# Routing seven of eight token tiles while the last tile is still in the mixers

## The chip, the core and the metric

The kernel runs on one core of a Trainium2 chip. The metric is the device time of one execution in microseconds. The engines are named as in the profile: PE (matmul), PEld (its weight loads), DVE (vector), ACT (scalar), POOL (GpSimd), SP (the engine that issues most DMAs); "q" behind a name is its sequencer.

## What is computed

One layer over 1024 prompt tokens and 8 sample tokens, width 1024, float32. The trunk: norm, one input projection to 3740 columns, three groups of recurrent heads, output projection, residual. Then a mixture of experts: the reference's router takes the best of 4 groups and in it the best 2 of 8 experts, each a SwiGLU of width 256.

```python
h2 = _rms_norm(x, norm2_g[li]).reshape(b * l, D_MODEL)
pg = jax.nn.softmax((x @ rg_w + rg_b).astype(F32), axis=-1)   # x is h2 here
pg_top, g_idx = lax.top_k(pg, 1)
le = (x @ re_w + re_b).astype(F32).reshape(t, N_GROUPS, EXP_PER_GROUP)
...
v2, i2 = lax.top_k(pe, TOP_K)
```

The experts' outputs, weighted by the gates, are added to x, and a last norm follows.

## The kernel before

**Trunk.** The 1024 tokens go through in 8 tiles (0 to 7) of 128. The engines' programs are written by hand, with a semaphore for each step. `body(t)` of each engine does tile t's mixers and, woven into them, the input projection of tile t+1 (`unit`) and what is left of tile t-1: output projection (`project_out`), `residual`, `norm2`, the transposes of the normed rows (`turn_h2`, `put_h2T`), the router's matmul (`route`) and its bias (`logits`), which leaves 36 logits per token in `lg`. In tile 7 there is no next tile; its loop over levels (`order`, with steps P, lin and TU) passes between PE, DVE, ACT and POOL. The 8 sample tokens go along, in tile 7 under names in `_s`. Behind `body(7)` stand tile 7's own output projection, residual, norm, transposes, router and the store of its normed rows (`store_h2`) to `h2_d` in HBM. All engines then meet at a barrier.

**Routing.** In `experts`, a first block starts the weights of experts 0 to 3 on SP and routes all 9 tiles at once on DVE, with `then` after nearly each instruction (it waits for its own result): `first_max` finds a first maximum in five instructions; one-hot rows `oh`; counts and positions of each token within its expert by matmuls with triangular and all-one matrices (L2065 to L2071); experts ranked by their count; the rank's place looked up (L2177 to L2181); an address of each token-slot; one-hots of tile and row (L2205 to L2209), and 18 matmuls (L2094) that scatter the token numbers into a table, `tokens`.

**Experts.** 23 "quads" of 128 slots hold the ranked experts: the first 8 ranks have 128 slots each, the next 12 have 96, the last 12 have 64; what goes beyond is left to a loop of overflow tiles at the end, whose number DVE puts into a table in `overflow_table` during quad 1. For each quad POOL gathers rows from `h2_d` (L2249), PE transposes them (L2405), multiplies by w1 and w3 (`mm1`, L2416), DVE and ACT form the gated hidden rows, PE turns them (L2423) and multiplies by w2 (`mm2`, L2435), POOL scatters to `y2_d`. SP waits for the first two gathers, then loads the experts' weights of ranks 4 to 31 in order into 7 buffers, each as soon as the quads that used it are done. A last phase adds the two outputs per token, norms and stores.

## Time before and its profile

| | |
|---|---|
| runs | 1418.8, 1418.57, 1414.5 us; median 1418.57 us |
| profiled execution | 1419.8 us, of which the span shown is 1418.0 us |
| PE busy in the span | 1253.5 us (88%) |
| DVE busy | 636.3 us (45%) |
| ACT, POOL busy | 396.9 us (28%), 472.0 us (33%) |
| granted PE clock, mean | 0.932 of full |

Times in the rows are microseconds from the span's start. The trunk lasts to about 1035, routing to 1073, the quads to 1371, the last phase to 1418. A share near 1.00 in the column "DMA share" means that all 16 DMA engines are taken.

### The profile page before, as it was taken

The numbers are of one execution on the slowest core, as the hardware profiler recorded it, in microseconds if no ns is written. First come the engines' busy times: TensorE is split into PE (matmuls) and PEld (weight loads), VectorE is DVE, ScalarE is ACT, GpSimd is POOL, SyncE is SP. The second block draws the span as 40 slices with busy tenths as digits, with TensorE's granted clock in tenths as the row PEclk, the third lists the DMA queues.
The fourth block names the chain that finished last, engine by engine and source line by source line (L and its number), as shares of the span: only waits on it lengthen the run. The fifth ranks groups of instructions, "written<-read, shape, count | busy, mean of one in ns | idle before, by whom it ended". The sixth has DMA issues, their size and how long they took to land. (4 is left out here: it accounts for less than half of the span.)

```text
span 1418.0 us, 32185 instructions
## 1 busy us (share of the span) xinstructions
PE 1253.5 (88%) x13694; PEld 951.6 (67%) x13694; DVE 636.3 (45%) x1372; ACT 396.9 (28%) x832; POOL 472.0 (33%) x398
## 2 busy tenths in 40 slices
PE   7988899999999999999999999978645999998860
PEld 6778689879879978978987978756533333333320
DVE  2748763355256246246245444445353322222228
ACT  3233134234234224223423422322100222221113
POOL 1615582372264145336238238233001111111100
PEclk9999999999999999999999999967857999999985
DMA  9887637836935844853873662580076979999968
GB/s 270 266 222 213 194 98 242 253 106 197 282 122 166 274 128 151 264 186 106 250 230 106 201 197 85 180 90 19 13 312 262 359 304 413 416 417 416 395 228 318
DMA packets 217735, 317.28 MB, mean 224 GB/s; under 512 B 15332, under 2 KB 187952, under 8 KB 209000
## 3 DMA queue, kind: packets, MB, share of 16 engines
q1 hardware_dynamic: 205176, 277.51, 59.0%
q10 hardware_dynamic: 5792, 20.78, 4.3%
q0 software_dynamic: 6624, 16.92, 3.1%
q8 instruction: 110, 1.80, 0.6%
q14 instruction: 33, 0.27, 0.1%
HBM read 295.45 MB, written 27.01 MB: 227 GB/s over the span
## 5 line engine op out<-in xcount | busy, mean ns | idle before, releaser
L1566 PE MATMUL psum<-arena 128*128 128x256 f32 (+3 forms) x1536 | 309.7, 355 | 3.4 <-issue 3.4
L1566 PEld LDWEIGHTS psum<-arena 128*128 128x128 f32 x1536 | 253.9, 193 | 32.6 <-issue 4.1
L2416 PE MATMUL psum<-arena 128*64 128x512 f32 (+1 forms) x832 | 169.3, 619 | 8.1 <-DMA arena<-in_exp_w 8.1
L1562 PE MATMUL psum<-arena 128*128 128x128 f32 x1152 | 138.9, 281 | 3.6 <-DVE arena L1104 3.6
L1248 DVE COPY_PREDICATED arena<-arena,psum 128x128 f32<-128x128 int32 x280 | 85.7, 306 | 120.6 <-PE psum L1749 113.6
L1562 PEld LDWEIGHTS psum<-arena 128*128 128x128 f32 x1152 | 134.3, 196 | 6.3 <-issue 5.8
L674 POOL TENSOR_TENSOR arena<-arena 128x768 f32<-128x768 f32 (+1 forms) x32 | 59.2, 1850 | 197.9 <-ACT arena L902 197.9
L2416 PEld LDWEIGHTS psum<-arena 128*64 128x64 f32 (+1 forms) x832 | 51.9, 135 | 108.4 <-issue 106.1
L1836 PE MATMUL psum<-arena 128*128 128x256 f32 x512 | 117.5, 389 | 0.8 <-ACT arena L979 0.8
L1836 PEld LDWEIGHTS psum<-arena 128*128 128x128 f32 x512 | 98.8, 196 | 14.8 <-ACT arena L979 1.2
L2258 POOL DMA_INDIRECT y_d<-arena x23 | 23.0, 1002 | 221.8 <-DVE arena L2357 221.8
L2435 PE MATMUL psum<-arena 128*64 128x512 f32 (+1 forms) x416 | 83.2, 594 | 0.8 <-DVE arena L2374 0.8
L2363 DVE TENSOR_SCALAR arena<-psum 128x256 f32<-128x256 f32 x23 | 9.8, 425 | 154.3 <-PE psum L2416 154.3
L748 ACT ACTIVATE arena<-psum 128x256 f32<-128x256 f32 (+2 forms) x72 | 25.1, 348 | 179.3 <-PE psum L1566 179.3
L616 POOL TENSOR_TENSOR arena<-arena 128x1152 f32<-128x1152 f32 x24 | 67.0, 2792 | 1.9
L1749 PE MATMUL psum<-arena 32*64 32x64 f32 (+1 forms) x2400 | 60.9, 232 | 6.9 <-DVE arena L1248 6.2
L658 POOL TENSOR_TENSOR arena<-arena 128x768 f32<-128x768 f32 x8 | 16.5, 2068 | 139.5 <-DVE arena L1187 139.5
L1749 PEld LDWEIGHTS psum<-arena 32*64 32x64 f32 (+1 forms) x2400 | 49.6, 139 | 19.3 <-issue 8.8
L2435 PEld LDWEIGHTS psum<-arena 128*64 128x64 f32 (+1 forms) x416 | 25.6, 131 | 54.6 <-issue 53.6
L638 POOL TENSOR_TENSOR arena<-arena 128x384 f32<-128x384 f32 x16 | 18.0, 1142 | 129.6 <-DVE arena L1142 129.6
L2291 ACT ACTIVATE arena<-arena 128x256 f32<-128x256 f32 x23 | 9.6, 416 | 173.4 <-DVE arena L2363 173.4
L1506 PE MATMUL psum<-arena 64*64 64x64 f32 x1344 | 50.4, 229 | 6.1 <-DVE arena L1265 6.1
(402 smaller groups left out, 2025.1 us busy)
## 6 DMA issues: line engine op xcount, KB each, us to landing
arena<-in_w_in SPq DMA_DIRECT2D x96, 1024.0 KB, 6.5
arena<-in_exp_w SPq DMA_DIRECT2D x96, 1024.0 KB, 16.6
arena<-in_w_out SPq DMA_DIRECT2D x32, 1024.0 KB, 5.8
arena<-in_w_in SPq DMA_DIRECT2D x24, 512.0 KB, 5.0
arena<-y_d SPq DMA_DIRECT2D x16, 512.0 KB, 12.2
arena<-in_x_prompt ACTq DMA_DIRECT2D x15, 512.0 KB, 6.1
arena<-in_w_in SPq DMA_DIRECT2D x8, 576.0 KB, 4.7
arena<-in_w_in SPq DMA_DIRECT2D x8, 560.0 KB, 4.3
```

Source lines behind the costliest of these rows:

```text
L616: g.tensor_tensor(cv3, cv3, part, ALU.add).then_inc(step("tap" if i < 3 else "conv"), 1)
L674: g.tensor_tensor(near_z(zk[dt % 2][R, :]), near(e), near_qk(k), ALU.mult)
L748: ins = a(columns(w if w < QKV0 else w - CONV, n), src[:, 0:n], ACT.Copy)
L1248: ins = v.copy_predicated(h3(att_b)[:, h:h + 2, :], b3(q_mask[4 * half + j], 2, 64), new)
L1506: ins = mm(out[HALF[b ^ cross], 64 * h:64 * h + 64], lhs(h, b), rhs(h, b), start=True, stop=True)
L1562: ins = mm(b[:, j * P:(j + 1) * P], w[:, c, j * P:(j + 1) * P], hT[:, c, :], start=(c == 0), stop=(c == KC - 1))
L1566: ins = mm(b[:, 0:n], hT[:, c, :], w[:, c, 0:n], start=(c == 0), stop=(c == KC - 1))
L1749: ins = mm(bank[6 + i][HALF[b], 64 * j:64 * j + 64], left[R, at:at + 64], right[R, at:at + 64], start=True, stop=True)
L1836: ins = mm(bank[6 if b else 3][:, WIDE * (m % 2):WIDE * (m % 2) + WIDE], oT[:, c * P:c * P + P], w[:, c, :], start=(c == 0), stop=(c == KC ...
L2258: pool.indirect_dma_start(y2_d, bass.IndirectOffsetOnAxis(ap=idx[q % NX][1], axis=0), Y[q % NX], None, bounds_check=2 * (NT * P + NS) - 1, ...
L2416: ins = mm(bank[2 + q % 2][at:at + width, :].rearrange("p (m n) -> p m n", m=2), xT[q % 2][:, c, at:at + width], w13[n % NB][:, :, c, :], ...
L2435: ins = mm(bank[4 + 2 * (q % 2) + b][at:at + width, :], hT[q % 2][:, c * P + at:c * P + at + width], w2[n % NB][:, c, 512 * b:512 * b + 51 ...
```

## The change

- The router's matmul takes the rows before the norm: norm2_g is multiplied into the router's weights at the start (with its loads cut in halves, three more small DMAs), and `logits` multiplies by the row's reciprocal root. `turn_h2` transposes x2, not h2, so it no longer waits for the norm. At the end of the trunk `norm2(7)` comes behind the transposes on DVE and ACT.
- Tiles 0 to 6 and the sample tokens are routed during tile 7: first choices and second choices, total, keys, ranks, tables, positions, look-up, addresses, one-hots, in nine places of DVE's program, with their matmuls in four places of PE's. Experts are ranked by these tokens alone.
- Behind the barrier only tile 7's tokens are routed and placed, on top of what the psum banks hold. The table has 96 tiles, not 64, and a slot of tile 7 beyond its expert's room makes 32 more overflow tiles run. SP no longer waits for `by_rank`.

```diff
-OVER = 32
+SLOT_TILE = list(range(NT - 1)) + [NT, NT - 1]
+EARLY = NTT - 1
+OVER_EARLY = (2 * ((NT - 1) * P + NS)) // (2 * TS + 1)
+OVER = OVER_EARLY + N_EXP
 TILES = NQ + OVER
+TAB = 96
+assert TILES <= TAB
...
+PICK = (4, 8, 8, 8, 8, 1, 1)
+def first_max(v, then, iota, n, out, ap, k, top, cand, mi):
+    c = t3(cand[:, 0:n * k], k)
+    then(v.tensor_reduce(top, ap, AX, ALU.max))
+    then(v.tensor_tensor(c, ap, spread(top, k), ALU.is_ge))
+    then(v.scalar_tensor_tensor(c, c, -64.0, spread(iota[:, 0:k], n, 1), ALU.mult, ALU.add))
+    then(v.tensor_reduce(mi, c, AX, ALU.min))
+    then(v.tensor_tensor(t3(out, k), c, spread(mi, k), ALU.is_equal))
+def pick_first(v, then, lg, iota, n, best, scratch, tmp):
...
+    first_max(v, then, iota, n, ohk0, t3(sel, 8), 8, best, cand, mi)
+def pick_second(v, then, lg, iota, n, oh, second, scratch):
...
+    then(v.scalar_tensor_tensor(sel, ohk0, -1e30, sel, ALU.mult, ALU.add))
+    first_max(v, then, iota, n, ohk1, t3(sel, 8), 8, second, cand, mi)
+    oh4 = oh.rearrange("p (t k e) -> p t k e", k=2, e=32)
+    for k, ohk in enumerate((ohk0, ohk1)):
+        ins = tt(oh4[:, :, k, :].rearrange("p t (g e) -> p t g e", e=8), spread(t3(ohk, 8), 4, 2),
+                 spread(t3(ohg, 4), 8, 3), ALU.mult)
+    then(ins)
+    return lambda d4: tt(t3(d4, 4), lg[:, :, 0:4], spread(mx, 4), ALU.subtract)
+def look_up(v, then, n, words, oh, tabs, tmp, uw, uw_i, parts_i, parts):
+    w = n * words
+    for j in range(words):
+        ins = v.tensor_tensor(t3(tmp[:, 32 * n * j:32 * n * j + 32 * n], 32), t3(oh, 32), spread(tabs[:, 32 * j:32 * j + 32], n, 1), ALU.mult)
+    then(ins)
+    then(v.tensor_reduce(uw, t3(tmp[:, 0:32 * w], 32), AX, ALU.add))
+    then(v.tensor_copy(uw_i, uw))
+    v.tensor_scalar(parts_i[:, 0:w], uw_i, PACK - 1, None, ALU.bitwise_and)
+    then(v.tensor_scalar(parts_i[:, w:2 * w], uw_i, PACK.bit_length() - 1, None, ALU.logical_shift_right))
+    then(v.tensor_copy(parts, parts_i))
...
+def addresses(v, then, n, pos, parts, columns, addr_i, place_i, place, late=None):
+    tt, ts, stt = v.tensor_tensor, v.tensor_scalar, v.scalar_tensor_tensor
+    far, over, addr, step_up, past, idx, more, shift = pieces(columns, *[n] * COLUMNS)
+    if late is None:
+        first, second, cap32, ovb = pieces(parts, *[n] * 4)
+    else:
+        first, second, behind, cap32, ovb, n_early = pieces(parts, *[n] * 6)
+    ts(far, pos, float(2 * TS), None, ALU.is_gt)
...
+    if late is not None:
+        stt(more, n_early, float(P), idx, ALU.mult, ALU.is_lt)
+    stt(step_up, step_up, -float(2 * TS), far, ALU.add, ALU.mult)
+    then(stt(past, ovb, float(P), idx, ALU.mult, ALU.add))
+    if late is not None:
+        stt(shift, behind, -1.0, more, ALU.add, ALU.mult)
+    then(tt(addr, addr, step_up, ALU.add))
+    if late is not None:
+        v.tensor_reduce(late, more, AX, ALU.add)
+        then(stt(past, shift, float(P), past, ALU.mult, ALU.add))
+    then(stt(past, past, float(NQ * P), addr, ALU.add, ALU.subtract))
+    then(tt(past, past, over, ALU.mult))
...
+    then(v.tensor_copy(place, place_i))
...
-                     (rw_g, A["router_g_w"][0].rearrange("(p c) n -> p (c n)", c=KC)),
-                     (rw_e, A["router_e_w"][0].rearrange("(p c) n -> p (c n)", c=KC))]
+                     (g2c.rearrange("p (b c) -> p b c", b=2), A["norm2_g"][0].rearrange("(b p c) -> p b c", b=2, c=KC // 2))]
+            for b in range(2):
+                half = slice(D // 2 * b, D // 2 * b + D // 2)
+                loads += [(rw_g[:, 16 * b:16 * b + 16], A["router_g_w"][0, half].rearrange("(p c) n -> p (c n)", c=KC // 2)),
+                          (rw_e[:, P * b:P * b + P], A["router_e_w"][0, half].rearrange("(p c) n -> p (c n)", c=KC // 2))]
...
             def norm2(t):
                 done(act, "x2", t)
                 freed(act, "h2", t)
+                freed(act, "lg", t)
...
             put_oT(NT - 1)
+            put_h2T(NT - 1)
             norm2(NT - 1)
             store_x2(NT - 1)
-            put_h2T(NT - 1)
             store_h2(NT - 1)
             for name in ("x2_stored", "tail_stored"):
...
+                if last:
+                    early_first(0, EARLY - 2)
+                    early_second(0, EARLY - 2)
...
                     if what == "lin":
+                        if last and m == 0:
+                            early_first(EARLY - 2, EARLY)
+                        if last and m == 4:
+                            early_second(EARLY - 2, EARLY)
+                            early_total()
+                        if last and m == 6:
+                            early_keys()
+                        if last and m == 7:
+                            early_ranks()
+                        if last and m == 9:
+                            early_tables()
...
+                if last:
+                    early_positions()
...
+                if last:
+                    look_up(v, then, E2, 2, e_oh, tabs, e_pair, e_uw, e_uw_i, e_parts_i, e_parts)
...
-                tt(lg[:, 36 * t:36 * t + 36], bank[7][:, 0:36], rb, ALU.add).then_inc(step("lg"), 1)
+                v.scalar_tensor_tensor(lg[:, 36 * slot_of(t):36 * slot_of(t) + 36],bank[7][:, 0:36], st2[:, 2:3], rb, ALU.mult, ALU.add).then_inc(step("lg"), 1)
...
+            def early_first(a, b):
+                if b == EARLY:
+                    done(dve, "s_lg", 0)
+                pick_first(v, then, lg3[:, a:b, :], iota, b - a, best[:, a:b], e_scratch[:, 0:sum(PICK) * (b - a)], e_tmp)
+            def early_second(a, b):
+                scratch = e_scratch[:, 0:sum(PICK) * (b - a)]
+                oh = e_oh[:, 64 * a:64 * b]
+                gap = pick_second(v, then, lg3[:, a:b, :], iota, b - a, oh, second[:, a:b], scratch)
+                oh4 = oh.rearrange("p (t k e) -> p t k e", k=2, e=32)
+                if b == EARLY:
+                    then(ts(oh4[:, b - a - 1, :, :], oh4[:, b - a - 1, :, :], cum[:, NS - 1:NS], None, ALU.mult))
+                tt(t3(e_S[:, 32 * a:32 * b], 32), oh4[:, :, 0, :], oh4[:, :, 1, :], ALU.add)
+                then(gap(d4[:, 4 * a:4 * b]))
+            def early_total():
+                v.tensor_reduce(e_total, e_S.rearrange("p (t e) -> p e t", e=32), AX, ALU.add).then_inc(step("e_total"), 1)
+            F = slice(0, N_EXP)
+            key_col, rank, cap, n_ov, ex_col, n_ex = (e_cols[F, n:n + 1] for n in range(6))
+            def early_keys():
+                done(dve, "e_count_mm", 0)
+                v.scalar_tensor_tensor(key_row[F, :], bank[4][F, 32:64], 32.0, key_lead[F, :], ALU.mult, ALU.add)
+                then(cp(n_ex, bank[4][F, 0:1]))
+                then(v.scalar_tensor_tensor(key_col, n_ex, 32.0, lead_col[F, :], ALU.mult, ALU.add))
...
+                then(v.tensor_reduce(n_ov, ovm[F, :], AX, ALU.add))
+                ts(ovT[F, :], ones[F, :], n_ov, None, ALU.mult)
+                ts(ovT_b[F, :], ones[F, :], n_ov, -float(PACK), ALU.mult, ALU.mult)
+                then(ts(ovT_p[F, :], ones[F, :], n_ov, float(PACK), ALU.mult, ALU.mult))
...
+            def early_positions():
+                for b in range(2):
+                    T4 = slice(half * b, half * b + half)
+                    for k in range(2):
+                        ins = tt(tmp4[:, T4, k, :], oh4[:, T4, k, :], t3(bank[4 + b][:, 384:512], 32), ALU.mult)
+                then(ins)
+                then(v.tensor_reduce(e_pos, t3(e_tmp, 32), AX, ALU.add))
+                dve.sem_inc(step("e_pos"), 1)
+            def early_hot():
+                tile3, slot3 = t3(e_tile_hot, TAB), t3(e_slot_hot, P)
+                then(tt(tile3, spread(iota[:, 0:TAB], E2, 1), spread(e_place[:, 0:E2], TAB), ALU.is_equal))
+                tt(tile3, tile3, spread(dst_f[:, 0:E2], TAB), ALU.mult)
+                for half in range(2):
+                    N = slice(EARLY * half, EARLY * half + EARLY)
+                    tt(slot3[:, N, :], spread(iota, EARLY, 1), spread(e_place[:, E2 + N.start:E2 + N.stop], P), ALU.is_equal
+                       ).then_inc(step("e_hot"), 1)
...
             put_oT(NT - 1)
+            addresses(v, then, E2, e_pos, e_parts, e_columns, e_addr_i, e_place_i, e_place)
+            early_hot()
             residual(NT - 1, 0)
             residual(NT - 1, 1)
+            put_h2T(NT - 1)
             norm2(NT - 1)
-            put_h2T(NT - 1)
             logits(NT - 1)
             done(dve, "lg", NT - 1)
...
+                        if last and m == 3:
+                            early_counts()
+                        if last and m == 4:
+                            early_positions()
+                        if last and m == 5:
+                            early_tables()
...
+            def early_counts():
+                done(pe, "e_total", 0)
+                mm(bank[4][F, 0:1], e_total, ones[:, 0:1], start=True, stop=True)
+                mm(bank[4][:, 32:64], ones, e_total, start=True, stop=True).then_inc(step("e_count_mm"), 1)
+            def early_positions():
+                half = EARLY // 2
+                done(pe, "e_above", 0)
+                for b in range(2):
+                    o, at = bank[4 + b][:, 384:512], 32 * half * b
+                    mm(o, cum, e_S[:, at:at + 128], start=True, stop=False, skip_group_check=True)
+                    for i in range(half * (b + 1) - 1):
+                        n = max(i + 1 - half * b, 0)
+                        mm(o[:, 32 * n:128], ones, spread(e_S[:, 32 * i:32 * i + 32], half - n, 1), start=False,
+                           stop=(i == half * (b + 1) - 2), skip_group_check=True)
+                mm(bank[4][F, 64:96], ones[F, F], above[F, :], start=True, stop=True).then_inc(step("e_rank_mm"), 1)
+            def early_tables():
+                done(pe, "e_rank", 0)
+                mm(bank[5][:, 0:32], first_b[F, :], of_rank[F, :], start=True, stop=True)
...
+                mm(bank[5][0:1, P:P + 32], e_cols[F, 4:5], ident[F, F], start=True, stop=True).then_inc(step("e_tabs_mm"), 1)
+            def early_places():
+                done(pe, "e_pos", 0)
+                done(pe, "oc_dn", NT - 1)
+                mm(bank[5][:, 0:32], ones, e_total, start=True, stop=False, skip_group_check=True)
+                for n in range(E2):
+                    done(pe, "e_hot", 0, n // EARLY + 1)
+                    mm(bank[4][0:TAB, 0:P], e_tile_hot[:, TAB * n:TAB * n + TAB], e_slot_hot[:, P * n:P * n + P],
+                       start=(n == 0), stop=False, skip_group_check=True)
...
             def turn_h2(t):
-                done(pe, "h2", t)
-                hv = h2.rearrange("p (t c) -> p c t", c=KC)
-                for c in range(KC):
-                    ins = tr(bank[c // 4][:, (c % 4) * P:(c % 4 + 1) * P], hv[:, c, :], ident)
+                for b in range(2):
+                    done(pe, "x2" if b else "x2a", t)
+                    xv = x2[:, 512 * b:512 * b + 512].rearrange("p (t c) -> p c t", c=KC // 2)
+                    for c in range(KC // 2):
+                        ins = tr(bank[b][:, c * P:(c + 1) * P], xv[:, c, :], ident)
...
             project_out(NT - 1, 1)
+            early_places()
             turn_h2(NT - 1)
             route(NT - 1)
...
+            mm(bank[5][:, 0:32], cum, S, start=False, stop=True, skip_group_check=True).then_inc(step("pos_mm"), 1)
+            pe.wait_ge(step("hot"), 1)
+            for n in range(2):
+                ins = mm(bank[4][0:TAB, 0:P], tile_hot[:, TAB * n:TAB * n + TAB], slot_hot[:, P * n:P * n + P],
+                         start=False, stop=(n == 1), skip_group_check=True)
             ins.then_inc(step("places_mm"), 1)
+            mm(bank[6][:, 0:1], ones, late, start=True, stop=True).then_inc(step("late_mm"), 1)
             pe.wait_ge(step("places"), 1)
-            mm(bank[5][:, 0:64], places, fold, start=True, stop=True).then_inc(step("table_mm"), 1)
+            mm(bank[5][:, 0:TILES], places[0:TAB, :], ident[0:TAB, 0:TILES], start=True, stop=True).then_inc(step("table_mm"), 1)
...
+            pick_first(v, then, lg[:, EARLY:NTT, :], iota, 1, m1[:, EARLY:NTT], scratch, tmp)
+            gap = pick_second(v, then, lg[:, EARLY:NTT, :], iota, 1, oh, m2[:, EARLY:NTT], scratch)
+            tt(S, oh[:, 0:32], oh[:, 32:64], ALU.add).then_inc(step("S"), 1)
+            gap(d4[:, 4 * EARLY:4 * NTT]).then_inc(step("d4"), 1)
+            look_up(v, then, 2, 3, oh, tabs, tmp, uw, uw_i, parts_i, parts)
+            dve.wait_ge(step("pos_mm"), 1)
+            then(tt(t3(tmp[:, 0:64], 32), t3(oh, 32), spread(bank[5][:, 0:32], 2, 1), ALU.mult))
+            then(red(pos, t3(tmp[:, 0:64], 32), AX, ALU.add))
+            addresses(v, then, 2, pos, parts, columns, addr_i, place_i, place, late)
+            for j in range(2):
+                v.scalar_tensor_tensor(tile_hot[:, TAB * j:TAB * j + TAB], iota[:, 0:TAB], place[:, j:j + 1],
+                                       dst_f[:, 2 * EARLY + j:2 * EARLY + j + 1].to_broadcast([P, TAB]), ALU.is_equal, ALU.mult)
+                ins = ts(slot_hot[:, P * j:P * j + P], iota, place[:, 2 + j:3 + j], None, ALU.is_equal)
+            ins.then_inc(step("hot"), 1)
+            tt(m2, m2, m1, ALU.subtract).then_inc(step("d12"), 1)
...
+            v.tensor_copy(places[0:TAB, :], bank[4][0:TAB, 0:P]).then_inc(step("places"), 1)
+            dve.wait_ge(step("late_mm"), 1)
+            then(v.tensor_copy(ov_exp[:, OV - 1:OV], bank[6][:, 0:1]))
             dve.wait_ge(step("table_mm"), 1)
...
                 sp.wait_ge(step(f"xg_in{u}"), 16)
-            sp.wait_ge(step("by_rank"), 1)
...
             def overflow_table():
-                for b in range(OVER // 8):
...
+                any_late, n_early, steps = ov_exp[0:1, OV - 1:OV], ov_end[0:1, 31:32], iota[0:1, 0:OV - 1]
+                then(v.tensor_scalar(any_late, any_late, 0.0, float(N_EXP), ALU.is_gt, ALU.mult))
+                then(v.tensor_tensor(any_late, any_late, n_early, ALU.add))
+                then(v.tensor_copy(ov_exp_i[0:1, OV:OV + 1], any_late))
+                for b in range(OV // 8):
+                    then(v.tensor_tensor(ov_le, spread(ov_end, 8, 1), spread(iota[:, 8 * b:8 * b + 8], 32), ALU.is_le))
                     then(v.tensor_reduce(ov_exp[:, 8 * b:8 * b + 8], ov_le, AX, ALU.add))
-                v.tensor_copy(ov_exp_i, ov_exp).then_inc(step("ov_table"), 1)
+                then(v.tensor_scalar(sel, steps, n_early, None, ALU.is_ge))
+                then(v.tensor_scalar(at, steps, n_early, -float(N_EXP), ALU.subtract, ALU.add))
+                then(v.tensor_tensor(at, at, sel, ALU.mult))
+                then(v.tensor_tensor(ov_exp[0:1, 0:OV - 1], ov_exp[0:1, 0:OV - 1], at, ALU.add))
+                v.tensor_copy(ov_exp_i[0:1, 0:OV - 1], ov_exp[0:1, 0:OV - 1]).then_inc(step("ov_table"), 1)
```

## Rows read from the trace of the kernel before

**Rows 1.** Windows of two stages: busy time (instructions) by engine, granted clock, DMA share, GB/s

```profile
1037.00:1080.00 43.00, 15.63 (x80) 13.14 (x81) 25.01 (x87) 1.73 (x3) 4.05 (x4) 0.54 0.77 308
...
1190.00:1240.00 50.00, 50.00 (x299) 18.78 (x299) 13.79 (x36) 10.46 (x22) 9.57 (x10) 1.00 1.02 416
```

**Rows 2.** The chain that ended last, behind the trunk: start us, us, what

```profile
1037.82 0.21 DVE arena L2120
...
1074.48 4.60 DMA arena<-h_d,arena
...
1083.91 9.15 PE psum L2416 x32
...
1292.33 25.18 DMA arena<-in_exp_w
```

**Rows 3.** Windows of short stretches

```profile
1022.00:1024.00 2.00, 2.00 (x11) 1.75 (x10) 0.00 (x0) 0.00 (x0) 0.00 (x0) 1.00 0.00 0
...
1117.00:1122.00 5.00, 5.00 (x30) 2.29 (x28) 3.27 (x11) 1.83 (x4) 1.00 (x1) 1.00 0.40 127
```

**Rows 4.** Timeline of DVE while it routes: start us, us, instruction

```profile
1059.13 0.75 DVE L2181 TENSOR_REDUCE arena<-arena 128x18 f32<-128x576 f32 x1
...
1061.26 0.18 DVE L2192 TENSOR_TENSOR arena<-arena 128x18 f32<-128x18 f32 x1
1061.47 0.18 DVE L2193 TENSOR_TENSOR arena<-arena 128x18 f32<-128x18 f32 x1
...
1065.07 1.36 DVE L2206 TENSOR_TENSOR arena<-arena 128x1152 f32<-128x1152 f32 x1
...
1073.34 0.28 DVE L2339 COPY arena<-arena 128x1 int32<-128x1 int32 x2 [0.34 <-DVE arena L2220]
```

**Rows 5.** Timeline of DVE in tile 7; in brackets what it waited before, and for whom

```profile
928.79 0.95 DVE L1174 TENSOR_REDUCE arena<-arena 128x12 f32<-128x768 f32 x1 [11.39 <-ACT arena L867]
...
955.66 1.31 DVE L1248 COPY_PREDICATED arena<-arena,psum 128x128 f32<-128x128 int32 x4 [3.04 <-PE psum L1749]
...
968.49 1.33 DVE L1248 COPY_PREDICATED arena<-arena,psum 128x128 f32<-128x128 int32 x4 [4.25 <-PE psum L1749]
...
976.20 1.32 DVE L1248 COPY_PREDICATED arena<-arena,psum 128x128 f32<-128x128 int32 x4 [3.81 <-PE psum L1749]
...
998.05 0.56 DVE L1288 TENSOR_TENSOR arena<-arena,psum 128x384 f32<-128x384 f32 x1 [3.23 <-PE psum L1809]
...
1017.52 0.69 DVE L1327 TENSOR_TENSOR arena<-arena,psum 128x512 f32<-128x512 f32 x1 [9.90 <-PE psum L1836]
```

**Rows 6.** Timeline of PE in tile 7

```profile
937.20 1.97 PE L1846 MATMUL psum<-arena 128*128 128x128 f32 x8 [1.74 <-DVE arena L1332]
941.13 1.04 PE L1861 MATMUL psum<-arena 8*128 8x8 f32 x8 [1.96 <-DVE arena L1416]
...
978.62 0.74 PE L1506 MATMUL psum<-arena 64*64 64x64 f32 x18 [1.80 <-DVE arena L1265]
```

**Rows 7.** Timeline of all engines, end of the trunk and placement matmuls

```profile
1028.23 1.97 PE L1846 MATMUL psum<-arena 128*128 128x128 f32 x8 [3.85 <-DVE arena L1332]
...
1030.25 0.33 ACTq L975 DMA_DIRECT2D h_d<-arena  x1
...
1034.71 0.20 DVE L1340 TENSOR_TENSOR arena<-psum,arena 128x36 f32<-128x36 f32 x1 [3.78 <-PE psum L1853]
...
1067.35 3.97 PE L2094 MATMUL psum<-arena 128*64 128x128 f32 x36 [10.93 <-DVE arena L2209]
```

**Rows 8.** Timeline of DVE and PE around the overflow table

```profile
1112.66 0.42 DVE L2322 TENSOR_REDUCE arena<-arena 128x8 f32<-128x256 f32 x1
...
1115.89 0.42 DVE L2363 TENSOR_SCALAR arena<-psum 128x256 f32<-128x256 f32 x1 [2.50 <-PE psum L2416]
...
1119.21 0.44 PE L2423 MATMUL psum<-arena 128*128 128x128 f32 x2
```

**Rows 9.** Summary of line 2249, the gathers of token rows (23 DMAs)

```profile
DMA to landing us min/median/max: 4.3/10.0/11.8
```

292 lines of the change are left out of this document (113 added, 179 removed).

## The prediction

> **What bounds the kernel now.** I read the page first, then the windows by stage, then the chain that ended last, then the timeline engine by engine around the end of the trunk. The windows show two regimes. In a stage like 1190 to 1240 PE is busy in all of it at the full clock and the DMA engines are taken too (share 1.02); between 1037 and 1080 PE works 15.6 of 43 us at 0.54 of the clock, DVE is the busiest, and DMA is idle for about 10 us (share 0.77) [rows 1]. There the kernel waits for the routing. The chain says the same: from 1037.8 it runs through DVE's short instructions, then 4.6 us of the first gather, then the first quad at 1083.9, and much later, at 1292, 25 us of expert weights [rows 2]. From the first routing instruction (1037.6, 0.2 before the chain's first row here) to the first token indices at 1073.34 [rows 4] are 35.7 us in which no matmul of the trunk or the experts runs. That is what the change attacks.
>
> **Does an earlier start reach the end?** The weights stream is saturated late on, so I ask whether it would swallow the gain. It has holes while the 7 buffers are full: one five-us window has a DMA share of 0.40, and there are two more such holes up to 1170 [rows 3]. A load behind them starts when a quad frees a buffer. So if the quads start earlier, the loads do too, and the late saturated stretch moves as a whole. The 10 us of idle DMA in front [rows 1] and some of the holes pay for it; all idle DMA time up to 1170, summed over such windows, is about 25 us, more than the gain below. I count the shift of the first `mm1` in full.
>
> **Routing that remains (term 1).** For one tile DVE issues: `pick_first` 12 chained instructions, `pick_second` 7 steps, the sum S 1, `look_up` 5, position 2, `addresses` 10, one-hots 1: 38 steps. A chained instruction of 18 elements costs 0.21 us from start to start (0.18 long) [rows 4]. 38 x 0.21 = 8.0. Some 15 more ride in a step without a wait, at half the price: 1.5. The reduce of 192 elements and the one-hots of 96 and 128 columns are longer: 0.5, by 0.75 us for 576 and 1.36 us for 1152 elements [rows 4]. Then four placement passes of PE; 36 took 3.97 us, two side by side, so 0.22 a pair [rows 7], and 96 columns no longer go side by side: 0.9, plus 0.2 of handover. From there to the indices before: last one-hot 1069.0, matmuls to 1071.4, indices at 1073.34, so 1.9 us unchanged. With 0.4 for the new waits: 13.4 us in place of 35.7. **-22.3 us** (bounds -20 and -24).
>
> [...]
>
> **The gather (term 2).** Before, the first gather left at 1074.48 onto idle queues and landed in 4.6 us [rows 2]. Now it leaves near 1053, while the first four experts' 12.6 MB (12 loads from 1037.5) are still coming until about 1068. The 23 gathers took 4.3 / 10.0 / 11.8 us to land [rows 9], nearly all beside weights. I take the median: 10.0. **+5.4 us** (bounds 0 and +7.2).
>
> **The overflow table (term 3).** It grows from 4 pairs of 0.42 + 0.42 us [rows 8] to 8 pairs, and by seven small instructions: 3.6 + 1.5 = +5.1 us on DVE in quad 1. DVE had 2.50 us to spare there [rows 8], so the hidden rows of quad 2 start 2.6 late. PE's turn of them (1119.21) had 0.6 to spare, since h was ready at 1118.6. **+2.0 us** (bounds 0 and +5.1).
>
> **Tile 7 (term 4).** PE waited 1.74 us for the norm and 1.96 for the sample's norm before the two transposes [rows 6]; both go. But the sums behind them need `put_h2T`, which DVE reaches only after nm and atd, so 2.3 of the 3.7 us remain. DVE's early work, by the prices above: first and second choices of six tiles 6.7 us in front of a wait of 11.39; first choices of the last two slots 2.6 in 3.04; second choices and total 2.8 in 4.25; keys 2.9 in 3.81 [rows 5]; ranks and tables about 1.0 in two waits of 1.6; positions 1.8 in a wait of 2.0; look-up 3.2 in 3.23; addresses and one-hots 8.8 in 9.90 [rows 5]. Some 30 us of work, each piece inside a wait for PE or ACT; without that cover it costs up to 30. PE's part is less covered: counts +0.2; positions, 1152 columns in two passes, 1.9 us plus the rank matmul at the full clock against a wait of 1.80 [rows 6]: +0.5 (at half the clock, +2.4); tables +0.5; look-up +0.1. Sum **-1.0 us** (bounds -2.3 and +8).
>
> **The end of the trunk (term 5).** Before, PE waited 3.85 us for residual and norm [rows 7]. Now it fills this with 34 placement passes. At the clock of 1.00 that it has at 1022 to 1024 [rows 3], each is 0.11: 3.7 us, to 1028.0; if the clock falls, 0.22 each: 7.5 us. The transposes then run warm, 1.0 instead of 1.97. But ACT's norm, 1.8 us, now stands behind its `put_h2T` (1029.6), DVE's scaling behind that (1.3), and the store of h2, issued at 1030.25 before [rows 7], at 1033.0. A lone store took 2.6 us to land: 1035.7. Before, the last thing was the logits at 1034.71 to 1034.9. **+1.0 us** (bounds -0.5 and +5). The barrier and the 2.7 us behind it stay.
>
> **The start (term 6).** Three more loads of about 0.45 us of SP's time ahead of the weights: +0.2.
>
> **Sum.** -22.3 + 5.4 + 2.0 - 1.0 + 1.0 + 0.2 = -14.7 us. The profiled execution took 1419.8 us (span 1418.0): 1405.1. The median of the runs shown is 1.2 lower, 1418.6, so 1403.9; I say 1404.
>
> **Rivals.**
> *The gather queues behind the weights.* If the rows only land when the four experts are in (about 1069), PE starts about 1069.5 instead of 1079.1, a shift of 9.6 instead of the 16.9 of terms 1 and 2; with the other terms 1411. For it: 12 loads are out. Against: gathers beside weights never took more than 11.8 us [rows 9]. [...] Chance 0.10.
> *DVE's early work is not covered.* The waits of 3.04, 3.81 and 3.23 us [rows 5] are within half a microsecond of the work put in, and what sticks out lengthens the ping-pong with PE. 8 us exposed give about 1413. Chance 0.08, of which 0.04 lies above 1414.
> *The clock comes back.* PE ran tile 7's middle at half the clock; two waits fewer could bring it back earlier, for up to 6 us: 1398. Against: it stayed low through 10 us of small matmuls without a wait. Or the gather lands as fast as before: 1399. Together 0.14.
> *The other side: one slot of tile 7 too many.* Ranks now come from 904 of 1032 tokens. If a single slot of tile 7 passes its expert's room, `overflow_table` adds 32 overflow tiles, each a gather (4.3 us at least [rows 9]), 3 MB of weights (7.5 us at 416 GB/s [rows 1]) and its matmuls, one after another: over 12 us each, about +400 us. It decides at the first such slot. I counted with the reference's router on its own inputs: ranks 0 to 7 end at most at 119 slots of 128, ranks 8 to 19 at 87 of 96, ranks 20 to 31 at 55 of 64. Chance 0.01.
> *Nothing changes*, since the weights bound the end. If the holes did not close, the saturated stretch would end where it does now, near 1418. Against: the holes [rows 3]. Chance 0.04.
> The forecast has 0.63, with a range of its own from 1399 to 1409.
>
> **Range and chances.** 1396 to 1413 takes in the fast gather, a slow one and most of an uncovered DVE. No change within 0.3% is 4.3 us, about what a measurement here can tell: 1414.3 to 1422.8. Faster 0.90; within it 0.07 (weights, and the worst of the uncovered work); slower 0.03 (the overflow slot, or more than 19 of the 30 us exposed).
>
> **What the profile after would show.** First gather about 16 us after the barrier's end, landing in about 10, PE's first transpose near 1062; SP's fifth expert at once behind; a new wait of about 2 us before L2423's counterpart in quad 2; in tile 7 no PE wait before the two transposes; placement passes of 0.11 us. Wrong, if the DVE waits of [rows 5] turn into PE waits, if the placement passes take 0.22, or if the wait for weights late on grows by what the start gained.

## The result and the profile after

The forecast was 1404 us with a range of 1396 to 1413. In the first comparison the kernel before took 1416.0 us and the changed one **1408.0 us** (medians of 22 runs each), ratio **0.9939** with an interval of [0.9923, 0.9956]: faster, within the range, 4 us above the forecast. A second set of runs of the same two kernels, made beside the experiments, gave 1417.4 and 1406.1, ratio 0.9912 [0.9881, 0.9944]. All runs of the two kernels in this study together have medians of 1417.4 (109 runs) and 1407.2 (29): 10.2 us.

The profiled execution after took 1415.2 us (span 1413.4), 7 us more than its own median; the one before took 1419.8. Their difference alone, 4.6 us, misleads, and the rows must be read from landmark to landmark.

The first stage of [rows 1] as a window of the kernel after (columns as there):

```profile
1050.00:1093.00 43.00, 17.96 (x74) 9.69 (x76) 14.05 (x75) 4.77 (x9) 6.03 (x6) 0.62 0.98 400
```

The DMA share behind the barrier rose from 0.77 to 0.98: nearly all of the idle DMA time there is gone. DVE is busy for 14 us instead of 25. The saturated stage, 1190 to 1240, is unchanged: PE busy in all 50 us at a clock of 1.00, DMA share 1.02. The first gather in the chain that ended last, for [rows 2]:

```profile
1064.71 9.36 DMA arena<-h_d,arena
```

DVE's timeline, for [rows 4]: the first routing instruction behind the barrier, one small step, and the first token indices.

```profile
1050.28 0.16 DVE L214 TENSOR_REDUCE arena<-arena 128x1 f32<-128x4 f32 x1 [5.09 <-PEq L311]
1050.47 0.16 DVE L215 TENSOR_TENSOR arena<-arena 128x4 f32<-128x4 f32 x1
...
1063.56 0.28 DVE L2494 COPY arena<-arena 128x1 int32<-128x1 int32 x2 [0.34 <-DVE arena L2367]
```

From 1050.28 to 1063.56 are 13.3 us (forecast 13.4, before 35.7), at 0.20 a chained step. The gather, 9.36 us at a DMA share of 1.02, takes twice what it took before (4.60 at 0.42).

Timeline of PE in tile 7, for [rows 6]: the two waits for the norm are gone. The matmuls for the positions (L2072, L2075; 2.8 us) and the tables (L2081 to L2088) stand in the ping-pong of PE and DVE, and the step behind them takes 1.40 us for 11 small matmuls at a granted clock of 0.50 (0.87 before, at 1.00):

```profile
990.42 0.40 PE L2081 MATMUL psum<-arena 32*128 32x32 f32 x2
...
996.60 1.40 PE L1941 MATMUL psum<-arena 64*64 64x64 f32 x11 [1.29 <-DVE arena L1421]
```

Timeline of all engines at the end of the trunk, for [rows 7]: 32 placement passes at 0.117 us each (clock 1.00) where a wait of 3.85 was, transposes in 1.13 us at 1.00 instead of 1.97 at 0.50, and the store of h2 at 1045.06.

```profile
1036.77 3.74 PE L2096 MATMUL psum<-arena 128*96 128x128 f32 x32
...
1040.35 1.13 PE L2128 MATMUL psum<-arena 128*128 128x128 f32 x8
...
1045.06 0.33 ACTq L1116 DMA_DIRECT2D h_d<-arena  x1
```

Timeline of DVE and then PE around the overflow table, for [rows 8]. DVE comes to quad 2 at 1113.27 without a wait, PE waits 2.03 us, and its eight transposes and 32 matmuls behind take 1.60 and 8.16 us at a granted clock of 0.60 and 0.86, against 1.05 and 7.09 at 1.00 in the quad ahead:

```profile
1113.27 0.42 DVE L2518 TENSOR_SCALAR arena<-psum 128x256 f32<-128x256 f32 x1
```

```profile
1102.47 1.05 PE L2560 MATMUL psum<-arena 128*128 128x128 f32 x8
1103.45 7.09 PE L2571 MATMUL psum<-arena 128*64 128x512 f32 x32
...
1116.00 0.44 PE L2578 MATMUL psum<-arena 128*128 128x128 f32 x2 [2.03 <-DVE arena L2524]
1116.28 1.60 PE L2560 MATMUL psum<-arena 128*128 128x128 f32 x8
1117.81 8.16 PE L2571 MATMUL psum<-arena 128*64 128x512 f32 x32
```

### The profile page after: what moved, and what is told of

It reads as the page before. It is cut to its first block and busy times, and to the rows that moved or that the text cites. A ratio compares the mean times of both kernels' runs of the same rounds, so it can differ in the third digit from the quotient of the medians.

```text
span 1413.4 us, 32307 instructions
## 1 busy us (share of the span) xinstructions
PE 1258.6 (89%) x13708; PEld 959.9 (68%) x13708; DVE 653.9 (46%) x1463; ACT 396.5 (28%) x832; POOL 472.3 (33%) x398
## 5 line engine op out<-in xcount | busy, mean ns | idle before, releaser
L1797 PE MATMUL psum<-arena 128*128 128x128 f32 x1152 | 142.2, 285 | 3.5 <-issue 2.0
L1043 ACT ACTIVATE arena<-psum 128x512 f32<-128x512 f32 (+1 forms) x64 | 34.6, 593 | 71.5 <-PE psum L1918 63.7
```

The lines of the kernel that those rows point to most:

```text
L1043: ins = a(E[dt % 2][0:DT_ROWS[dt], 512 * b:512 * b + 512], bank[b][0:DT_ROWS[dt], :], ACT.Exp)
L1797: ins = mm(b[:, j * P:(j + 1) * P], w[:, c, j * P:(j + 1) * P], hT[:, c, :], start=(c == 0), stop=(c == KC - 1))
```

## The experiments

Four landmarks carry the comparison, read from DVE's and PE's timelines: DVE's first step of tile 6 (the sum of squares, L1174 before, L1319 after), the first routing instruction behind the barrier, the first expert transposes, and the end of the span. The last two columns are the only places late in the quads where PE waits for weights: its wait ahead of `mm1`, and how long `mm1` then took, in quad 18 (32 matmuls) and in quad 19 (64). All in us:

| profile | tile 6 | barrier | transposes | end | barrier to end | quad 18 | quad 19 |
|---|---|---|---|---|---|---|---|
| kernel before | 817.1 | 1037.6 | 1079.1 | 1418.0 | 380.4 | 3.99, 8.40 | 4.08, 10.02 |
| before_again | 818.7 | 1036.3 | 1077.7 | 1414.9 | 378.6 | 3.88, 8.43 | 4.02, 8.38 |
| before_table_twice | 820.9 | 1037.5 | 1078.6 | 1418.2 | 380.7 | 4.13, 9.86 | 2.60, 7.07 |
| normless_alone | 816.5 | 1028.5 | 1069.6 | 1405.1 | 376.6 | 3.93, 10.07 | 2.31, 7.07 |
| kernel after | 826.0 | 1050.3 | 1074.1 | 1413.4 | 363.1 | 3.60, 9.96 | 2.89, 7.07 |
| after_again | 820.6 | 1038.1 | 1061.9 | 1401.1 | 363.0 | 3.65, 9.95 | 2.90, 7.07 |
| chain_12us_later | 824.9 | 1043.5 | 1078.1 | 1416.9 | 373.4 | 3.59, 9.79 | 3.06, 7.07 |
| table_spread | 819.6 | 1041.1 | 1064.9 | 1402.8 | 361.7 | 3.52, 8.43 | 4.37, 9.90 |
| positions_late | 823.8 | 1044.4 | 1068.4 | 1411.1 | 366.7 | 3.54, 8.58 | 4.26, 10.03 |
| spread_and_late | 822.0 | 1042.3 | 1066.1 | 1402.1 | 359.8 | 4.25, 9.90 | 2.66, 7.07 |
| two_behind_gather | 817.6 | 1037.1 | 1056.1 | 1396.5 | 359.4 | 3.99, 10.09 | 2.73, 7.07 |
| spread_and_gather | 820.3 | 1041.0 | 1060.5 | 1397.4 | 356.4 | 4.55, 10.03 | 2.81, 7.07 |
| spread_kept_warm | 819.8 | 1044.3 | 1068.1 | 1403.8 | 359.5 | 0.94, 7.09 | 3.38, 7.07 |
| both_kept_warm | 823.1 | 1043.9 | 1063.2 | 1400.1 | 356.2 | 1.66, 7.09 | 3.36, 7.07 |

Read the last two columns together, since two later readings hang on them. At a granted clock of 1.00 the two `mm1` take 7.09 and 7.07 us; what is above that is the lower clock behind a wait (over each `mm1` a mean of 0.82 to 0.84 where it took 8.4 to 8.6 us, and 0.70 to 0.72 where it took 9.8 to 10.1). Except where the waits were filled on purpose, the clock fell at the first wait in every profile, at two prices: `mm1` of quad 18 took either 8.4 to 8.6 us or 9.8 to 10.1. The two waits end 17.1 to 17.5 us apart in all of these, so a quad 18 that is slower only shortens the wait behind it. Behind 8.4 to 8.6 us the next wait was 4.02 to 4.37 and the clock fell again, which costs 1.3 to 3.0 us at the end; behind 9.8 to 10.1 it was 2.31 to 3.06 and the clock held. What decides between the two isn't settled. Both occur with the stall at the overflow table and without it.

Executions with the same trunk reached the barrier up to 13 us apart; from the barrier on, the two executions of the kernel before differ by 1.8 us and those of the changed kernel by 0.1. The theory at the start: the stall at the overflow table, the early work in tile 7 and a longer trunk took what the forecast had more. The rivals: the weights stream takes back every early gain, or the excess of the trunk is chance.

**table_spread**, the table in pieces (the three functions are the old one cut up; their bodies are left out here):

```
                 if q == 1:
-                    overflow_table()
+                    overflow_begin()
+                if 3 <= q < 7:
+                    overflow_pairs(q - 3)
+                if q == 7:
+                    overflow_end()
```

> The changed kernel with its overflow table cut up: two pairs of the table in each of quads 3 to 6 and the last five instructions in quad 7, nothing else moved. Theory A: the table cost PE a wait of 2.03 us ahead of turn_h in quad 2 and then 1.6 us at the lower clock, 3.7 us in all, and the quads set the end. Then that wait is gone and the run is 3 to 4 us faster than the changed kernel, about 0.9972 of it. Rival B: late on the weights stream sets the end and takes any gain of the early quads back; then mm1 of quad 4 starts 3.7 us earlier after the barrier but the end moves by less than 1 us.

It took 1403.7 us, 0.9885 [0.9836, 0.9934] of the kernel before, 2 to 4 us less than the changed kernel in its two sets of runs. PE's wait in quad 2 is gone and from quad 4 on the quads come 3.8 us earlier behind the barrier. The last two loads come 3.9 us earlier too: PE's wait for them ends 244.4 and 261.9 us behind the barrier, instead of 248.2 and 265.8. But from barrier to end only 1.4 us are left. PE's timeline shows where the rest went, at the two waits for weights. First the kernel after, then table_spread:

```profile
1298.51 9.96 PE L2571 MATMUL psum<-arena 128*64 128x512 f32 x32 [3.60 <-DMA arena<-in_exp_w]
...
1316.05 7.07 PE L2571 MATMUL psum<-arena 128*32 128x512 f32 x64 [2.89 <-DMA arena<-in_exp_w]
```

```profile
1285.44 8.43 PE L2580 MATMUL psum<-arena 128*64 128x512 f32 x32 [3.52 <-DMA arena<-in_exp_w]
...
1302.92 9.90 PE L2580 MATMUL psum<-arena 128*32 128x512 f32 x64 [4.37 <-DMA arena<-in_exp_w]
```

In quad 19 the same 64 matmuls take 2.8 us more behind the longer wait: PE idled, and ran them at a clock of 0.50 for the first 5 us and at 1.00 from 1308.9 on. The longer wait comes from quad 18, which was 1.5 us quicker here, and not from the missing stall: the wait ahead of quad 18 is the same (3.52 and 3.60), and spread_and_late, also without the stall, has the other pattern (2.66, then 7.07). The stream of weights didn't swallow the gain, so rival B fell. Of theory A the 3.7 us stand as far as the last load; in this one execution the clock took 2.8 of them back.

**chain_12us_later**, 60 idle chained steps:

```
+            for _ in range(60):
+                then(ts(tmp[:, 0:18], tmp[:, 0:18], 1.0, None, ALU.mult))
             pick_first(v, then, lg[:, EARLY:NTT, :], iota, 1, ...)
```

> The changed kernel with 60 more chained instructions of 18 elements ahead of the routing chain behind the barrier, 60 x 0.20 = 12 us that do nothing else. It asks what a microsecond of this chain is worth at the end. Theory A (as the prediction counted it: loads start when a quad frees a buffer, so all that follows moves as a whole): 12 us slower than the changed kernel. Rival B: the first four experts' weights still start at the barrier's end, and the late saturated stretch of the stream has slack against the quads, so only 4 to 8 us of the 12 show at the end.

1416.8 us, 0.9975 [0.9947, 1.0004]. The 60 steps took 14.1 us (1043.52 to 1057.65), 0.235 a step and not the 0.20 counted. The first transposes came 10.8 us later behind the barrier: the gather left later, with fewer weights in flight, and landed in 5.97 us instead of 9.36, so that PE's wait for it fell from 11.7 to 8.35 us. Of these 10.8 us, 10.3 reach the end. A microsecond of this chain is worth about 0.7 at the end, and what is lost goes to the gather, not to the late stream as rival B had it. Theory A holds from the transposes on, but not for the way to them.

**normless_alone**, on the kernel before, the router on x2 with what belongs to it (three more loads, `put_h2T` ahead of `norm2` at the end) and nothing else; cut to the main lines:

```
-                done(pe, "h2", t)
-                hv = h2.rearrange("p (t c) -> p c t", c=KC)
+                for b in range(2):
+                    done(pe, "x2" if b else "x2a", t)
+                    xv = x2[:, 512 * b:512 * b + 512].rearrange("p (t c) -> p c t", c=KC // 2)
...
-                tt(lg[:, 36 * t:36 * t + 36], bank[7][:, 0:36], rb, ALU.add).then_inc(step("lg"), 1)
+                v.scalar_tensor_tensor(lg[:, 36 * t:36 * t + 36], bank[7][:, 0:36], st2[:, 2:3], rb, ALU.mult, ALU.add).then_inc(step("lg"), 1)
```

> The kernel before with one part of the change alone: the router reads x2 without the norm (turn_h2 and turn_h2_s on x2, the norm's gain folded into the router's weights, the row's scale applied to the logits, three more loads, put_h2T ahead of norm2 at the end); routing stays behind the barrier as it was. In the profiles the trunk of the changed kernel had grown by 11.6 us before tile 7. Theory A: this part does it (transposes start as soon as residual is there, and the order of work on PE and DVE loses time in each tile): 6 to 12 us slower than the kernel before, with the barrier's end some 10 us later. Rival B: the growth is the stalls of single executions, for the two kernels alike: within 2 us of the kernel before, or 2 us faster since two waits in tile 7 go.

1412.0 us, 0.9947 [0.9917, 0.9977]. Theory A fell, and rival B's figure was too small: 7 us faster. Tile 6 starts at 816.5 in its one profile, so nothing shows that this part lengthens the trunk. From there to the barrier it takes 212.0 us instead of 216.6 to 220.5. PE's turn of tile 7 (`turn_o`) comes 72.5 us behind DVE's first step of the tile, instead of 74.6 to 76.1, and the wait of 3.85 us [rows 7] is 0.31.

**before_table_twice**, on the kernel before:

```
-                for b in range(OVER // 8):
+                for b in 2 * list(range(OVER // 8)):
...
+                for _ in range(7):
+                    then(v.tensor_copy(ov_exp_i, ov_exp))
```

> The kernel before with its overflow table in the size that it has after the change: eight pairs instead of four (the four twice) and seven more small chained instructions, all in quad 1. Theory A: a wait of about 2 us in quad 2 and the lower clock behind it, 3.5 us slower than the kernel before, 1.0025 of it. Rival B (weights set the end): within 1 us. Its trunk is that of the kernel before untouched, so its profile also shows how much a second execution of the same trunk differs from the first: by less than 1 us if the 11.6 us that the trunk grew belong to the change, by several us if they are chance.

1420.0 us, 0.9998 [0.997, 1.0026]. PE waits 1.98 us in quad 2, as theory A has it, and the waits for the last two loads end 3.5 us later behind the barrier than in the kernel before. The end didn't move, because this execution fell into the other pattern (9.86 in quad 18, then a wait of 2.60 and 7.07) and the kernel before's into the costly one. Against normless_alone, which has the same code behind the barrier as the kernel before and the same pattern as this run, the stall costs 4.1 us to the end (380.7 against 376.6). The interval of the ratio leaves room both for theory A's 1.0025 and for no change.

**after_again**: no edit.

> The changed kernel as it is, once more, for a second profile and for times beside the other variants on one chip. In the six profiles so far the time from DVE's first step of tile 6 to the first expert transpose was 262.0, 257.7 (kernel before and its variant) and 248.2, 245.4 (the changed kernel's), 14.5 us less on average, but the medians differ by 8.6. Theory A: tiles 0 to 6 grow by chance alone, by dips of the clock of 1.6 us in some tiles; then this profile has tile 6 starting between 816 and 821 us as often as later, and the ratio to the kernel before comes out near 0.990 (14 us). Rival B: something of the change makes the dips more frequent or the start later by some 5 us; then tile 6 starts at 822 or later again and the ratio stays at 0.994.

1406.1 us, 0.9912 [0.9881, 0.9944]; its profile has a span of 1401.1, 12.3 us less than the first one's, all of it ahead of the barrier. Windows of the same code in the kernel after, tiles 1 and 2, then in after_again:

```profile
246.05:364.03 117.98, 113.57 (x1346) 99.25 (x1345) 50.70 (x115) 38.16 (x80) 48.43 (x42) 0.99 0.58 185
364.03:477.98 113.95, 111.83 (x1346) 97.89 (x1345) 51.42 (x114) 38.16 (x80) 48.61 (x42) 1.00 0.60 191
```

```profile
244.46:360.02 115.56, 112.05 (x1346) 98.01 (x1345) 50.56 (x114) 38.16 (x80) 48.63 (x42) 1.00 0.61 189
360.02:475.87 115.85, 113.64 (x1346) 99.59 (x1345) 51.20 (x114) 38.16 (x80) 48.71 (x42) 0.99 0.61 189
```

Where the mean clock reads 0.99, PE is busy 1.5 to 1.8 us longer for the same 1346 matmuls. It hits tile 1 in one execution and tile 2 in the other. By the ten profiles with the changed trunk tile 6 starts at 821.7 on average (817.6 to 826.0), by the three with the old one at 818.9 (817.1 to 820.9). Most of the 12 us is chance; whether 3 us are the change's isn't settled.

**positions_late**, PE's position matmuls behind the last matmuls of tile 7, DVE's part behind `put_oT`:

```
                         if last and m == 4:
-                            early_positions()
+                            early_rank()
...
+            done(pe, "oc_dn", NT - 1)
+            early_positions()
             turn_o(NT - 1)
```

> The changed kernel with its matmuls for the early positions taken out of the middle of tile 7 (they stood between two steps of the ping-pong) and put behind the tile's last matmuls, where PE waits 6.2 us for DVE; DVE's part of the positions follows put_oT, in front of the addresses, beside project_out. In the middle only the small rank matmul stays. Theory A (PE's early work in tile 7 costs 5.3 us instead of the 1.3 forecast: 2.4 for passes that no wait covers, 2.9 since the clock is low from 976 to 992 where without this work it is full): M7 to turn_o falls from 80.7 by 2.4 to 5.3 us and the end by as much. Rival B: the time is lost to DVE's early work, which this leaves in place: less than 1 us.

1407.5 us, 0.992 [0.9889, 0.9952]: no gain over the changed kernel. First PE's timeline of this kernel, then POOL's and DVE's around the last matrices of the keys:

```profile
981.32 1.23 PE L1741 MATMUL psum<-arena 64*64 64x64 f32 x18 [4.32 <-DVE arena L1421]
```

```profile
976.70 1.81 POOL L815 TENSOR_TENSOR arena<-arena 128x768 f32<-128x768 f32 x1 [1.50 <-ACT arena L1043]
976.77 1.82 DVE L1594 TENSOR_SCALAR arena<-arena 32x128 f32<-32x128 f32 x1
```

With some 2.8 us of matmuls out, the wait behind them is 4.32 instead of the 1.56 of table_spread: PE waits for DVE, whose keys took 4.9 us (973.96 to 978.86), where the forecast had 2.9. Of that, 1.55 us are one instruction, which took 1.82 us while POOL's ran over the same stretch. In six of the ten profiles with early routing the two don't meet, and it took 0.27; in the other four they do, and it took 1.82 or 1.83. So DVE's side bounds this step, as rival B has it, in an execution where DVE was held up. In spread_and_late, where it wasn't, the step with the positions out took 4.2 us instead of the 5.3 of the kernel after (from one group of 48 matmuls to the next, L1759), but `turn_o` gained at most 0.8 us by it. `turn_o` came 75.6 us behind the tile's first step (77.0 in spread_and_late), against 74.4 to 77.9 with the positions in place, and the position matmuls now stand just ahead of it. (The 80.7 of the expectation is where the output projection starts, 2.8 us behind `turn_o`.)

**spread_and_late**: both edits.

> Both edits together on the changed kernel: the overflow table cut up over quads 3 to 7, and the positions' matmuls behind tile 7. If both theories hold and add up, 3.7 + 2.4 to 5.3 us; less what the last load of weights takes back: with the table spread PE waited 4.37 us for it instead of 2.89 and ran the matmuls behind at half the clock, 9.9 instead of 7.07 us. I expect 4 to 7 us faster than the changed kernel, 0.995 to 0.997 of it.

1403.6 us, 0.9904 [0.9869, 0.9939]. From barrier to end 359.8 us, 3.2 less than the changed kernel: with the table spread and the clock holding in quad 19 (7.07 behind a wait of 2.66), nearly all of the 3.7 us reach the end.

**two_behind_gather**, two experts' loads first:

```
-            for e in range(AT_ONCE):
+            for e in range(2):
                 load_w(sp, e, e)
...
+            sp.wait_ge(step("xg_in0"), 16)
+            for e in range(2, AT_ONCE):
+                load_w(sp, e, e)
```

> The changed kernel, but only two experts' weights (6 loads) leave at the barrier's end; experts 2 and 3 follow when the first gather has landed. Quads 0 and 1 need experts 0 and 1 alone. Theory A (the gather's 9.4 us are the weights beside it, the term of 5.4 us): it lands in 4 to 5 us after its issue and the first transposes come 4 to 5 us earlier against the barrier. Rival B: the gather takes as long anyway, being 128 rows of 4 KB one after another. For the end: the stream of weights pauses about 4 us. By the prediction's view (all moves with the quads) 4 us faster; if the stream sets the end, the wait for weights near 1300 grows by the pause, and the end is the same or up to 3 us later.

1403.6 us, 0.9893 [0.9852, 0.9934]. From barrier to transposes 19.0 us instead of 23.8. PE's timeline:

```profile
1056.06 1.97 PE L2562 MATMUL psum<-arena 128*128 128x128 f32 x8 [6.89 <-DMA arena<-h_d,arena]
```

The wait is 4.8 us shorter, and the gather landed in 4.53 us instead of 9.36 (4.60 before, [rows 2]), at a DMA share of 0.92 instead of 1.02. So theory A holds: the weights in flight beside it are what made the gather slow. Of the 4.8 us, 3.6 reach the end.

**before_again**: no edit.

> The kernel before as it is, once more, for a third profile of its trunk beside seven of the changed kernel's. DVE's first step of tile 6 stood at 817.1 and 820.9 us in the two profiles of the kernel before's trunk, and between 817.6 and 826.0, 822.0 on average, in the seven of the changed kernel's. Theory A (chance alone): this one lies anywhere between 817 and 826, and from barrier to end it takes 380.2 us within 1, or 3 less if the wait for the last weights stays under 3 us. Rival B (the change lengthens the trunk by some 4 us in the mean): it lies at 817 to 820 again.

1417.6 us. Identical code gave 1.0034 [1.0005, 1.0063] against its twin: here an interval is not to be trusted to a third of a per cent. From barrier to end 378.6 us.

**spread_and_gather**: table spread and two experts behind the gather.

> The changed kernel with the overflow table cut up over quads 3 to 7 and with experts 2 and 3 loaded behind the first gather; the positions stay in tile 7. From the barrier to the end the changed kernel took 363.1 and 363.0 us, with the table spread 361.7 (2.9 of it the lower clock behind the last wait for weights), with two experts behind the gather 359.4. Theory A: the two add up, since one shortens the way to the first quad and the other the way from quad 2 on: 355 to 358 us, and some 5 to 8 us faster than the changed kernel, 0.985 to 0.989 of the kernel before. Rival B: the stream of weights, which pauses 4 us, then sets the end: the two waits for weights near 1290 grow by what the quads gain, the clock falls behind them, and the stage takes 359 us or more.

**1398.1 us, 0.9886 [0.9856, 0.9915]**, and 356.4 us from barrier to end: the two add up, nearly (6.6 us less than the changed kernel's stage). The quads come 7.5 us earlier and the last loads 6.6: here the loads begin to lag behind the quads.

**spread_kept_warm**, both waits for weights filled:

```
-                for c in range(KC):
-                    ins = tr(...)
+                for _ in range(4 if q in (19, 20) else 1):
+                    for c in range(KC):
+                        ins = tr(...)
```

> The kernel with the overflow table spread, and with the eight transposes ahead of the two waits for weights (those of quads 19 and 20) done four times over instead of once: 3.1 us of work with the same result inside each wait, so that PE idles for about 1 us instead of 3.5 to 4.4. Over ten profiles mm1 of quad 19 took 7.07 us behind waits of 2.6 to 2.9 us and 9.90 to 10.02 behind waits of 4.0 to 4.4. Theory A (the idle time lets the clock fall, and this took back 2.9 of the 3.7 us that spreading the table gained): mm1 of quad 19 takes 7.07 and from the barrier to the end it is 361.7 - 2.9 = 358.8 us or up to 1 more. Rival B (the clock is low there for another reason, such as the DMA load): 9.9 again and 361 to 362 us.

1401.5 us, 0.9874 [0.982, 0.9929]. PE's timeline:

```profile
1299.58 3.68 PE L2570 MATMUL psum<-arena 128*128 128x128 f32 x32
1306.64 7.07 PE L2581 MATMUL psum<-arena 128*32 128x512 f32 x64 [3.38 <-DMA arena<-in_exp_w]
```

7.07 again, and 359.5 us from barrier to end: theory A. The end alone wouldn't show it, since spread_and_late has 359.8 without the filling. Quad 18 does: in all twelve profiles without it PE idled 3.5 to 4.6 us there and its `mm1` took 8.4 to 10.1 us at a clock of 0.70 to 0.84, in the two with it PE idled 0.94 and 1.66 us and it took 7.09 at 1.00, with the same loads in flight (DMA share 1.02 or 1.03 in all fourteen). It was the idle time, not the DMA load.

**both_kept_warm**: the same in spread_and_gather.

> The same filling of the two waits in the kernel with the table spread and experts 2 and 3 behind the gather, which took 356.4 us from the barrier to the end. There the clock fell in mm1 of quad 18 (10.03 us) and not in that of quad 19 (7.07, wait 2.81). Theory: the moment at which the last weights land sets the end, and what is lost ahead of it in quad 18 is only taken from the next wait; so mm1 of quad 18 gets back to about 7.1 us, the wait of quad 19 grows by as much, and the end does not move: 356 to 357 us. Rival: the quads set the end, 353 to 354 us.

1401.4 us, 0.9879 [0.9824, 0.9933], and 356.2 us. The matmuls of quad 18 fell from 10.03 to 7.09, and the wait of quad 19 grew from 2.81 to 3.36, on top of 2.7 us of added transposes. The moment at which the last weights land sets the end there: the 2.9 us that quad 18 saved don't come out at the end.

## Why the prediction was right, and where its terms were off

**Term 1, the chain** (-22.3): measured 35.7 to 13.3, **-22.4**. **Term 2, the gather** (+5.4): 4.60 to 9.36, **+4.8**, shown by two_behind_gather. Together the way from the barrier to the transposes went from 41.4 (three profiles) to 23.8 us: -17.5 where -16.9 stood. "The late saturated stretch moves as a whole" held as well: behind the barrier `mm1` of quads 17, 18 and 19 starts 14.2, 14.6 and 14.3 us earlier than before, which is about the 17.5 less the stall of term 3.

**Term 3, the overflow table** (+2.0): the stall was right (2.03), the term was mis-sized, since the lower clock behind it (0.60 and 0.86) adds 0.6 and 1.1: **+3.7** by quad 4, and by spread_and_late 3.2 of it at the end.

**Not in the sum: the clock at the last waits.** In the kernel before, the lower clock cost 3.0 us in quad 19 in one profile, 1.3 in a second, and nothing in normless_alone, which has the same code there; in the two profiles of the kernel after it didn't. That makes **-1.4** on average, and it is luck as far as is known: positions_late lost 3.0 us there with the stall in place, table_spread 2.8 without it.

**Terms 4 and 5, tile 7 and the end of the trunk** (-1.0 and +1.0): from tile 6 to the barrier it took 218.2 us before (mean of three) and 221.0 after (mean of the eight with the positions in place): **+2.8**. It divides into +1.2 in tile 6 (108.9 to 111.7 us before, 109.0 to 114.6 after, so perhaps chance), +1.7 from tile 7's first step to `turn_o` (75.6 to 77.3), and -0.1 from there to the barrier (32.1 to 32.0). So term 5 came out a little better than forecast, and term 4, forecast as a gain, was a loss. Taking the norm out gave 6.2 us by normless_alone, about what its two parts, 2.3 of waits and the hole of 3.85, add up to. All the early work costs 9.0 against that one profile, where the terms implied 6.2. The largest part that the rows show is an assumed clock: "the full clock" held for the positions and the placement (1.00 for both), but behind the tables it was low in six of eight executions (0.50, L1941 at 1.40 us, `turn_o` 77.8 to 77.9 us behind the tile's first step) and full in two (1.00, 0.82 us; 76.6 and 74.4). The kernel after and after_again run alike to 53.3 us behind tile 7's first step and are 3.5 us apart at `turn_o`; that is what the lower clock costs. A smaller part is DVE held up beside POOL, 1.55 us in four of ten executions, which no term had.

**Term 6, the start** (+0.2): up to tile 6 the mean rose by **2.8**, with ranges that overlap; 0.9 of it stands at the start of tile 0. This stays open.

From barrier to end it took 378.5 us before (mean of the three profiles with the old code there) and 363.1 after: -15.5, where -17.5, +3.7 and -1.4 make -15.2. The measured parts sum to 2.8 + 2.8 - 15.5 = -9.9 us, beside -10.2 by the medians of all runs and -14.7 by the forecast. The forecast was right by its main mechanism, the routing and the gather. Around it term 3 was too hopeful by 1.7 us, terms 4 and 5 together by 2.8 and term 6 by up to 2.6, and the clock of quad 19 hid 1.4 of that.

**The rivals.** The gather did not queue behind the weights: in the profile after it landed at 1074.07, and behind it, from 1074.1 to 1077.2, before SP issued the next load (1077.20), the DMA share was still 1.07 at 431 GB/s. The clock came back earlier in tile 7 in three of the eight executions (the group of 48 matmuls at 33.6 us took 0.93 us at a clock of 1.00 instead of 1.56 at 0.50), but fell again two steps later, and `turn_o` came no earlier; it held to the end of the tile's small matmuls only in after_again. No overflow tile ran. That the weights bound the end was wrong as a whole (chain_12us_later: 10.3 of 10.8 us behind the first transposes came through) and right at one place, between the last two loads.

## What to carry to other kernels

The long chain of small instructions was priced well by counting it (13.4 us forecast, 13.3 measured), though the 60 idle steps took 0.235 us each where 0.20 was counted. What is lost is lost where it moves to: ask what clock the borrowed cover leaves behind (0.50 behind the tables in six of eight executions), and not only whether it is long enough. Where PE waits for a load late in a kernel, look for the same instructions at two durations (here 7.07 and 8.38 to 10.03 us), and compare kernels at a landmark ahead of it too: with one profile each, table_spread and before_table_twice looked like mirror images, and it took all fourteen to see that the two patterns come with and without the stall. And when one profile after disagrees with the medians, profile it again before explaining it.

## What was unexpected of the hardware

- The 64 matmuls of quad 19 took 7.07 us at a granted clock of 1.00 behind waits of 2.31 to 3.38 us, and 8.38 to 10.03 at 0.84 to 0.70 behind waits of 4.02 to 4.37. The 32 of quad 18 took 8.4 to 8.6 us in four profiles and 9.8 to 10.1 in eight, behind waits of 3.52 to 3.99 us in the four and 3.59 to 4.55 in the eight.
- The same trunk, run again, reached the barrier at 1050.3 and at 1038.1 us. Single tiles take about 2 us longer at a mean clock of 0.99, and one of chain_12us_later took 120.8 us at 0.96, where 114.0 is usual.
- A gather of 128 rows took 4.60 us with no weights in flight (DMA share 0.42) and 9.36 beside four experts' weights (1.02); with half of these held back it took 4.53 (0.92).
- A DVE instruction on 32x128 elements took 0.27 us alone and 1.82 or 1.83 when POOL's multiplication of 128x768 elements started just ahead of it; both then ended within 0.1 us of each other.
